# State-space angles made on POOL beside the feed-forward up stages and stored in DRAM; the direct products' table loads issued one piece ahead

## The reference

```python
# end of layer 0
x = x + squared_relu_mlp(rms_norm(x, norm_ffn[0]), ffn_up[0], ffn_down[0])   # 2048 -> 8192 -> 2048
# start of layer 1
u = rms_norm(x, norm_mix[1]) @ odd_w_in                 # 2048 x 2048
lam_bar = exp(lam * dt)                                 # one complex number per group and state
b_bar = ((lam_bar - 1) / lam)[..., None] * complex(b_re, b_im)
# states s[t] = lam_bar * s[t-1] + b_bar u[t];  y = Re(C s[t]) + d * u
z = gelu(y);  out = z * sigmoid(z @ w_glu + b_glu)
```

## Time and profile before

| | us |
|---|---|
| median of 3 runs | 4051.99 |
| lowest, highest | 4051.15, 4053.29 |
| the profiled execution's own time | 4037.2 |
| its span | 4035.9 |
| TensorE busy | 3800.0 (94%) |
| VectorE busy | 2590.0 (64%) |
| GpSimd busy | 1482.6 (37%) |
| ScalarE busy | 1790.8 (44%) |

### The profile page before, as it was taken

The page is one execution under the profiler, slowest core; times in us unless marked ns, Lnnn a source line. Parts: engine busy times, 40 slices in busy tenths (PEclk is TensorE's granted clock), DMA queues, the critical chain, the costliest instruction groups (busy, mean ns, idle before and its releaser), DMA issues.

```text
span 4035.9 us, 66394 instructions
## 1 busy us (share of the span) xinstructions
PE 3800.0 (94%) x28364; PEld 3232.6 (80%) x28364; DVE 2590.0 (64%) x3604; ACT 1790.8 (44%) x2785; POOL 1482.6 (37%) x710
## 2 busy tenths in 40 slices
PE   6898999998998999989999999999879989999998
PEld 3786888787877887888778888888768878888887
DVE  0435743785368897669879667885746876455457
ACT  1435443644355444445544444444435553333334
POOL 0332343233322441004344444444634434444443
PEclk8999999999999999999999999999899999999999
DMA  9653665355542442015356465657334435444543
GB/s 394 266 225 146 247 253 210 139 190 190 219 188 107 183 176 111 23 57 197 138 182 236 185 232 198 231 195 290 124 129 193 182 131 188 188 188 188 188 185 128
DMA packets 60663, 748.78 MB, mean 186 GB/s; under 512 B 6976, under 2 KB 9152, under 8 KB 16720
## 3 DMA queue, kind: packets, MB, share of 16 engines
q1 hardware_dynamic: 48960, 696.74, 45.2%
q0 software_dynamic: 9344, 45.69, 3.0%
q10 hardware_dynamic: 2064, 2.10, 0.1%
HBM read 727.65 MB, written 16.84 MB: 184 GB/s over the span
## 4 chain that ended last, share of the span: by engine, by line
PE 76%; DVE 13%; ACT 6%; DMA 3%; issue 2%; POOL 1%; SPq 0%; another core or an unknown queue 0%; DVEq 0%; ACTq 0%; POOLq 0%
PE ps L370 42%; PE ps L371 21%; DVE pieces L323 2%; DMA ring<-in_ada 2%; ACT pieces L307 2%; PE ps L2229 2%; PE ps L790 2%; DVE opa L571 1%; DVE r L1173 1%; PE ps L1899 1%; DMA s5u<-in_s5bt 1%; PE ps L3596 1%; DVE scr L592 1%; PE ps L3566 1%; PE ps L1044 1%
## 5 line engine op out<-in xcount | busy, mean ns | idle before, releaser
L370 PE MATMUL ps<-opa,pieces 128*128 128x512 f32 x6192 | 2250.1, 406 | 60.8 <-DVE pieces L323 36.5
L341 POOL TENSOR_TENSOR pieces<-ring,pieces 128x1024 fp32r<-128x1024 f32 x539 | 1345.1, 2496 | 2200.3 <-ACT pieces L307 2188.2
L371 PE MATMUL ps<-opa,pieces 128*128 128x256 f32 x6192 | 1740.1, 281 | 0.0
L307 ACT ACTIVATE pieces<-ring 128x1024 fp32r<-128x1024 f32 (+1 forms) x1110 | 1098.4, 1036 | 814.4 <-PE ps L371 813.9
L370 PEld LDWEIGHTS ps<-opa,pieces 128*128 128x128 f32 x6192 | 1171.3, 189 | 354.7 <-issue 40.6
L371 PEld LDWEIGHTS ps<-opa,pieces 128*128 128x128 f32 x6192 | 1177.6, 190 | 9.0 <-issue 5.3
L370 PE MATMUL ps<-opb,pieces 128*128 128x512 f32 x2560 | 907.9, 396 | 19.6 <-DVE pieces L323 13.8
L323 DVE TENSOR_TENSOR pieces<-ring,pieces 128x1024 fp32r<-128x1024 f32 (+1 forms) x571 | 724.5, 1269 | 272.0 <-ACT pieces L307 268.9
L371 PE MATMUL ps<-opb,pieces 128*128 128x256 f32 x2560 | 724.8, 283 | 0.0
L370 PEld LDWEIGHTS ps<-opb,pieces 128*128 128x128 f32 x2560 | 482.1, 188 | 141.4 <-issue 16.0
L371 PEld LDWEIGHTS ps<-opb,pieces 128*128 128x128 f32 x2560 | 482.6, 189 | 0.1
(11 more groups left out here) (425 smaller groups left out, 3345.2 us busy)
## 6 DMA issues: line engine op xcount, KB each, us to landing
ring<-in_up SPq DMA_DIRECT2D x64, 2048.0 KB, 7.7
ring<-in_down SPq DMA_DIRECT2D x64, 2048.0 KB, 7.7
ring<-in_win SPq DMA_DIRECT2D x56, 2048.0 KB, 7.7
ring<-in_ada SPq DMA_DIRECT2D x48, 2048.0 KB, 12.1
ring<-in_wout SPq DMA_DIRECT2D x24, 2048.0 KB, 7.7
ring<-in_evin SPq DMA_DIRECT2D x18, 2048.0 KB, 7.8
ring<-in_evout SPq DMA_DIRECT2D x8, 2048.0 KB, 8.0
ring<-in_xkv SPq DMA_DIRECT2D x8, 2048.0 KB, 7.6
```

Of the source, the lines that this page charges most:

```text
L307: a.do.activation(K.parts_of(p)[0][:, s, :], w[:, s, :], ACT.Copy).then_inc(*K.hi.up((p, h)))
L341: g.do.tensor_tensor(lo[:, s, :], w[:, s, :], hi[:, s, :].bitcast(F), ALU.subtract).then_inc(*K.lo2.up(p))
L370: pe.do.matmul(b[:, 0:512], hi[:, k, :], op[:, 512 * k:512 * k + 512], start=i == 0, stop=False)
L371: t = pe.do.matmul(b[:, 0:256], lo[:, k, :], half(op, 0, k), start=False, stop=i == kt - 1)
```

## The change

The angles are made earlier, and each is stored in DRAM. `pool_s5_angle` now makes one step's angles (256 elements) in two turns: a multiply and a two-operation rounding add (what ACT did before), then the subtraction of the large number, the difference, and a 128 KB store into a new DRAM tensor `s5_angles`. Its scratch is `cross5`, which DVE's table products use too. `pool_s5_beside` takes one turn after each `pool_feed` with t//16 equal to 2 or 4, the second and third up stages: 8 angles in each. A new angle waits until the store of the one before has landed. DVE's table products wait for angles 7 and 15 at two places, POOL for DVE's at two. ACT loads the angles back by pairs (`act_s5_angle`), and no longer makes `act_s5_whole`. POOL's queue in `pool_s5` holds only the products p.

Three smaller parts: the first direct product's tables are loaded at t = 112, the start of the last down stage's pieces, where they were loaded after the last one; the loads for the third and fourth direct product stand one piece earlier on POOL; and the first `pe_s5_in` comes after tile 12, the second waits for DVE's tile 13 only, with the PSUM banks handed out to fit.

```diff
+T_AFTER_ANGLES = {(2, 1, 0): 7, (4, 0, 1): 15}
+T_BEFORE_ANGLES = {0: (2, 0, 1), 8: (4, 0, 0)}
+def pool_s5_angle(K, n):
+    g = K.g
+    aq, at = K.cross5[:, 0:256], K.cross5[:, 256:512]
+    if n == 0:
+        g.wait_ge(*K.load["io5"].of("io5"))
+        g.wait_ge(*K.dve.of("ph"))
+    else:
+        g.wait_ge(*K.turned.of(("angle5", n - 1)))
+    if n in T_BEFORE_ANGLES:
+        g.wait_ge(*K.dve.of(("table", *T_BEFORE_ANGLES[n])))
...
+    g.do.tensor_tensor(r3(aq, 4), four, turn, ALU.mult).then_inc(*K.gps.up())
+    g.wait_ge(*K.gps.now())
+    g.do.tensor_scalar(at, aq, 1.0, MAG, ALU.mult, ALU.add).then_inc(*K.gps.up())
+    yield
+    g.wait_ge(*K.gps.now())
+    g.do.tensor_scalar(at, at, -MAG, None, ALU.add).then_inc(*K.gps.up())
+    g.wait_ge(*K.gps.now())
+    g.do.tensor_tensor(aq, aq, at, ALU.subtract).then_inc(*K.gps.up())
+    g.wait_ge(*K.gps.now())
+    g.do.dma_start(K.D["s5an"][n // 2][:, 256 * (n % 2):256 * (n % 2) + 256], aq).then_inc(*K.turned.up(("angle5", n), 16))
+    yield
+def act_s5_angle(K, m):
+    a = K.a
+    if m >= 2:
+        a.wait_ge(*K.act.of(("sin", 2 * m - 3)))
+    a.do.dma_start(K.an5[m % 2], K.D["s5an"][m]).then_inc(*K.load["an%d" % (m % 2)].up(("an", m), 16))
@@ def dve_s5_table(K, j):
+            if (j, c, h) in T_AFTER_ANGLES:
+                v.wait_ge(*K.turned.of(("angle5", T_AFTER_ANGLES[j, c, h])))
@@ def pool_s5_beside(K):
+    angles = chain.from_iterable(pool_s5_angle(K, n) for n in range(16))
     for t in range(2, 128):
...
+        if t == 112:
+            kept_all(K, g)
+            load_k(K, g, 2)
         pool_feed(K, p + t)
+        if t // 16 in (2, 4):
+            next(angles)
@@ def pool_odin(K):
-    kept_all(K, g)
-    load_k(K, g, 2)
...
     load_k(K, g, 3)
-    pool_feed(K, p + 5)
+    pool_feed(K, p + 4)
     g.wait_ge(*K.prod.of(("K", 3)))
     load_k(K, g, 1)
-    pool_feed(K, p + 8)
+    pool_feed(K, p + 7)
     g.wait_ge(*K.prod.of(("K", 1)))
     load_k(K, g, 0)
     pool_feed(K, p + 11)
-    pool_s5_angle(K, 0)
...
-    pool_s5_angle(K, 1)
@@ def pe_odin(K):
-        if n == 11:
+        if n == 12:
...
             pe_s5_in(K, 0)
@@ def act_odin(K):
-        if n in (12, 13):
-            act_s5_whole(K, n - 12)
+        if n == 10:
+            a.wait_ge(*K.prod.of(("K", 0)))
+            a.wait_ge(*K.turned.of(("angle5", 15)))
+            act_s5_angle(K, 0)
+            act_s5_angle(K, 1)
...
+        if n == 14:
+            act_s5_angle(K, 2)
@@ def pe_s5(K):
+    K.pe.wait_ge(*K.dve.of(("u", 13)))
+    pe_s5_in(K, 1)
     K.pe.wait_ge(*K.dve.of(("u", 15)))
-    pe_s5_in(K, 1)
@@ def act_s5(K):
-        if n % 2 == 0:
-            act_s5_whole(K, n // 2)
         act_s5_tables(K, n)
+        if n % 2 and n < 13:
+            act_s5_angle(K, n // 2 + 2)
@@ def pool_s5(K):
     for n in range(16):
-        if n % 2 and (n + 3) // 2 < 8:
-            pool_s5_angle(K, (n + 3) // 2)
```

More of the change, by code:

```diff
@@ L4 @@
 from contextlib import ExitStack
+from itertools import chain
 F = mybir.dt.float32
@@ L147, in begin @@
         for s in [self.tile, self.prod, self.hi, self.lo, self.lo2, self.act, self.dve, self.gps, self.stored,
-                  *self.landed, *self.kept, *self.load.values()]:
+                  *self.landed, *self.kept, self.turned, *self.load.values()]:
             s.n = 0
@@ L3204, in dve_s5_columns @@
     tt(fi, fi, ph2, ALU.mult, "fi")
+T_AFTER_ANGLES = {(2, 1, 0): 7, (4, 0, 1): 15}
[10 more added lines that the diff above has]
+        g.wait_ge(*K.dve.of(("table", *T_BEFORE_ANGLES[n])))
+    four = in_fours(K.io5)[:, :, 0][:, None, :].broadcast_to([P, 4, 64])
+    turn = of_step(K.ph5, n)[:, 0, :, None].broadcast_to([P, 4, 64])
+    g.do.tensor_tensor(r3(aq, 4), four, turn, ALU.mult).then_inc(*K.gps.up())
[14 more added lines that the diff above has]
+    a.do.dma_start(K.an5[m % 2], K.D["s5an"][m]).then_inc(*K.load["an%d" % (m % 2)].up(("an", m), 16))
 def dve_s5_table(K, j):
@@ L3225, in dve_s5_table @@
     if j:
-        v.wait_ge(*K.dve.of(("table", j - 1)))
+        v.wait_ge(*K.dve.of(("table", j - 1, 1, 1)))
     if j >= 2:
@@ L3236, in dve_s5_table @@
             v.wait_ge(*K.dve.now())
+            if (j, c, h) in T_AFTER_ANGLES:
+                v.wait_ge(*K.turned.of(("angle5", T_AFTER_ANGLES[j, c, h])))
             v.do.tensor_tensor(T, src[1 - c][:, s], b[:, s], ALU.mult).then_inc(*K.dve.up())
             v.wait_ge(*K.dve.now())
-            v.do.tensor_tensor(dst[c][:, s], dst[c][:, s], T, ALU.add if c else ALU.subtract).then_inc(*K.dve.up(("table", j)))
+            v.do.tensor_tensor(dst[c][:, s], dst[c][:, s], T, ALU.add if c else ALU.subtract).then_inc(*K.dve.up(("table", j, c, h)))
             yield
@@ L3246, in act_s5_pads @@
     which, k = TABLES[j]
-    a.wait_ge(*K.dve.of(("table", j)))
+    a.wait_ge(*K.dve.of(("table", j, 1, 1)))
     a.wait_ge(*K.dve.of("half5"))
@@ L3436, in pe_odin @@
             pe_s5_direct(K, ORDER_K[n])
-        if n == 11:
+        if n == 12:
+            at = K.ps.index(K.bank["tile", K.first["odin"] + 10])
+            K.z5b = Banks([K.ps[i] for i in (3, 4, 5, 6, 7, at)])
+            K.y5b = Banks([K.ps[i] for i in range(3) if i != at])
             K.pe.wait_ge(*K.act.of(("K", 0)))
@@ L3495, in of_step @@
     return a.rearrange("p (m q) -> p q m", q=4)[:, n % 4:n % 4 + d, n // 4 * 4:n // 4 * 4 + 4]
[L3498 to L3506, removed]
-    turn = of_step(K.ph5, 2 * m, 2)[:, :, :, None].broadcast_to([P, 2, 4, 64])
-    g.do.tensor_tensor(K.aq.rearrange("p (d m k) -> p d m k", d=2, m=4), four, turn, ALU.mult).then_inc(*K.gps.up(("turn5", m)))
-    g.wait_ge(*K.act.of(("whole5", m)))
-    g.do.tensor_scalar(K.at5, K.at5, -MAG, None, ALU.add).then_inc(*K.gps.up())
-    g.wait_ge(*K.gps.now())
-    if m >= 2:
-        g.wait_ge(*K.act.of(("tab", 2 * m - 3)))
-    g.do.tensor_tensor(K.an5[m % 2], K.aq, K.at5, ALU.subtract).then_inc(*K.gps.up(("angle5", m)))
-def act_s5_whole(K, m):
-    K.a.wait_ge(*K.gps.of(("turn5", m)))
-    K.a.do.activation(K.at5, K.aq, ACT.Copy, scale=1.0, bias=MAG).then_inc(*K.act.up(("whole5", m)))
 def act_s5_tables(K, n):
     a, an, sq, c, rt = K.a, K.an5[n // 2 % 2][:, 256 * (n % 2):256 * (n % 2) + 256], K.sq5[n % 2], K.cs5[n % 3], K.rt5[n % 3]
-    a.wait_ge(*K.gps.of(("angle5", n // 2)))
+    a.wait_ge(*K.load["an%d" % (n // 2 % 2)].of(("an", n // 2)))
     if n < 3:
@@ L3532, in act_s5_tables @@
     a.do.activation(c[:, 256:512], an, ACT.Sin, scale=-6.283185).then_inc(*K.act.up())
-    a.do.activation(sq, an, ACT.Sin, scale=3.1415925).then_inc(*K.act.up())
+    a.do.activation(sq, an, ACT.Sin, scale=3.1415925).then_inc(*K.act.up(("sin", n)))
     a.wait_ge(*K.act.now())
```

5 lines of the change are left out of this document (3 added, 2 removed).

## The result

| | before | changed |
|---|---|---|
| median of 20 runs, us | 4048.9 | 4058.8 |
| lowest, highest | 4036.99, 4054.46 | 4051.16, 4067.88 |
| the profiled execution, its span | 4037.2, 4035.9 | 4054.04, 4052.7 |

The ratio is 1.0023, with a 95% interval of 1.0016 to 1.0031: slower. The medians differ by 9.9 us; the interval means 6.5 to 12.6. The profiled execution of before lies 11.7 under its median and that of the changed kernel 4.8, so the two traces differ by more (16.8) than the kernels do. Most of the surplus of 6.9 will be found in one step of the output stage.

The account below looks back on a forecast made before the run. TensorE, 76% of the chain, was taken as the bound, so its waits count. Gains of 7.6 us against a loss of 11.6 gave +4.0: 4041 for the profiled execution, 4056 us as median, range 4045 to 4066.

Parts of the forecast that it names:

- The loads, 5.8: Direct products: earlier loads remove TensorE waits of 3.2 and 1.4 us and 1.2 of slow clock, a 5.8 us gain.
- The scan, 1.8: Output stage: with angle operations gone from between the products p, the first output step starts 1.8 us sooner.
- fourth rival: The scan's gain of 1.8 us goes only to another TensorE wait; within the range, no separate chance given.
- The clock in the second input step: Second input step, after the wait for its table: stays at half clock, 13.58 us where the first took 7.30.
- rival 2: Clock does not fall in the table wait, 2 us more gained; with early stores and no loss 4042, chance 0.08.
- Moving the input steps: First input step after tile 12, second after DVE's tile 13: costs nothing and changes nothing while the table lands last.
- The store's landing: Up stages: an angle store issued in mid-slab lands with the slab, 7.8 us after the split's end, or slightly later.
- The one-input operation: POOL's operation in the store's turn: hardly holds DVE up, unlike a two-input one, so it costs 0.
- The loss, 5.8 a stage: Second and third up stages: new angles waiting for stores lengthen POOL's loop, 11.6 us for two; bounds 0 to 19.
- slack of 1.4: Up stages: room in the POOL and DVE loop at the stage's start, 1.4 us, used up before anything is lost.
- Rival 3: POOL's loop costs more, from an excess of 1.6 us a pair: 16 us and more, 4060 to 4067, chance 0.23.
- The turn with a store costs 0: Up stages, odd tiles: one-input add, difference and store right after POOL's split cost 0.

Follow-up runs that it names:

- e2_loads: The kernel before with only the moved loads of the direct products, angles as before; 4042.1 us, ratio to before 0.9982.
- e11_loads: The same kernel as e2_loads, timed again in a later batch; 4042.4 us, ratio to before 0.9986.
- e3_late: The changed kernel with the direct products' loads back where they were before; 4061.7 us, ratio to before 1.0032.
- e9_turn_after: e1_swap with the new angle's multiply also waiting for DVE's square of the tile just ended; 4042.2 us, ratio to before 0.9984.
- e1_swap: The changed kernel with scratch halves swapped from angle to angle, the store's wait moved ahead of the odd tile's one-input operation; 4050.8 us, ratio to before 1.0007.
- e5_late_turn: e1_swap with the multiply waiting for DVE's square one tile too early, so it started as before; 4054.6 us, ratio to before 1.0010.
- e7_phase: The changed kernel with angle turns one tile later, stores issued in tiles without a slab's load; 4047.5 us, ratio to before 0.9996.
- e4_wait: The changed kernel without the multiply and first one-input operation of 14 angles, waits and stores kept; 4042.6 us, ratio to before 0.9987.
- e10_both: e7_phase with the multiply also waiting for DVE's square, no scratch swap; 4045.8 us, ratio to before 0.9992.

## Why the prediction was right, and where it was off

- **Direction: right; the size in part by luck.** 4056 was forecast and 4058.8 measured, but the forecast was +4.0 on a median of 4052.0, and the change was +9.9 on one of 4048.9. The kernel before came out 3.1 us lower than in its first three runs, and this hid half of what the sum missed. The loops that it named are the ones that the trace shows. (Its upper end of 4066 does not follow from a loss of 19 and a gain of 7.6, which give 4063; the time lies within either.)
- **The loads, 5.8: right**, 6.9 and 6.7 in e2_loads and e11_loads. In the traces the changed kernel comes to this stage 17.4 us late, reaches the first product 14.1 late (2781.78 against 2767.70), the third 11.1 late and the stage's last tile 10.0 late: 3.3 for the first wait, 3.0 for the slow clock and the second wait, 1.1 that I had not counted, of which e2_loads shows 0.6. The slabs that the loads passed lost nothing.
- **The scan, 1.8: right up to the first output step, and not shown beyond it.** Product to output is 19.4 to 21.4 us in the nine profiles with the angles elsewhere and 22.3 to 23.0 in the four without. But from the last tile of the input product to the next product's first tile it is 123.2 to 129.6 us in those nine and 121.5 to 128.3 in those four, with medians of 125.9 and 126.2. Nor do the medians of the times settle it. What is left for the scan when the loss and the loads' 6.8 (none in e3_late) are taken off is 2.9 us in e9_turn_after and 0 in e1_swap, and over all eight kernels with the angles elsewhere it runs from -2.5 (e5_late_turn) to 5.2 (e7_phase), with -0.6 for the changed kernel. The prediction's fourth rival, that this gain only goes to another wait, stays open.
- **The clock in the second input step: right.** It took 12.41 us and the granted clock was 0.52 from 2884 to 2894, the 1.2 GHz level; rival 2 did not come.
- **Moving the input steps: nothing, as said.** The second one now waits 2.76 us for DVE's scans (L3663) and not for its table; it starts 2.8 us after the last tile and started 2.4 after it before.
- **The store's landing: right in the middle, for the right reason.** 6.1 us, 8.2 after the split's end, beside the slab's 8.0. The Trainium skill's rule that an engine takes turns between its queues (DMA: Bandwidth & Descriptors, "Queues, rings and completion order") would have let it land early; 91 packets of the slab and none of the store's in 3.5 us do not agree, and only the last 38 of the slab's were mixed with them.
- **The one-input operation: right in size, and not for the reason given.** It cost DVE's two-input operation 0.08, the multiply 0.42. The prediction took the number of inputs to make the difference. By the rows of e1_swap it is the time that POOL's operation had left when the square began, 0.06 and 0.39. The Trainium skill's rule of the shared port pair (SBUF — State Buffer, "SBUF: two separate sides"), by which the one that starts first holds the pair for its whole instruction, agrees with both. The prediction let that rule cost 0.5 in each store's turn, 7 us in all; with the operation's 0.40 it would cost 0.06. Its own rows did not speak against the rule either: all eight of the L3510 took 1.49 us or more, so none shows what it takes alone. Twice 0.40 for its 512 elements would be an end at 2909.64, as the scans began; this is an estimate from L3227.
- **The loss, 5.8 a stage: mis-sized.** It was 8.0 with the down stage behind it (16.1 and 15.7 for two), and 7.8 and 6.6 in the up stages alone. The term that was too small is "the excess is 0.6 to 1.7 for each pair of tiles, 1.2 in the middle, in 6 pairs". The excess was 1.34 in most pairs (12.65 less 11.31; some took 12.4, one 13.0), and 7 angles of each stage wait, not 6: 9.4, and 8.0 when the slack of 1.4 is taken off. That is an upper value for the up stages; the next term was not in the sum at all. Rival 3 asked for an excess of 1.6, which did not come; its loss of 16 did, through the seventh pair and the down stages.
- **A term that was missing: the first tiles of the down stage.** There DVE's table operations ran beside POOL's splits, and TensorE waited for DVE's split. Timeline of POOL and DVE in the changed kernel, then TensorE's waits from 2306 to 2340 (before, 0.6 in one wait):

```profile
2318.20 2.45 POOL L342 TENSOR_TENSOR pieces<-ring,pieces 128x1024 fp32r<-128x1024 f32 x1 [0.36 <-ACT pieces L308]
2318.43 2.77 DVE L3280 TENSOR_TENSOR mix<-mix,scr 128x512 f32<-128x512 f32 x1
...
2323.76 2.92 DVE L3280 TENSOR_TENSOR mix<-mix,scr 128x512 f32<-128x512 f32 x1
```
```profile
PE ps L371 <- DVE pieces L324: 2.2, 2, 1.6
```

  L3280 took 2.8 and 2.9 us, and 0.69 in the same place of the kernel before. It costs 0.7 to 1.1 a stage and stays in the mildest variants: by TensorE's timeline the down stages take 1.1 us longer each in e4_wait and e9_turn_after, which is most of what these two lose. The wait for angle 7 was not it: the first table operation (L3278, 2315.50) followed DVE's split without a pause. Which of the two engines' operations starts first decides here, 0.23 us apart; that it comes out otherwise than before was seen and not changed by an experiment. The prediction gave "0, at worst 2 each" to this place for that wait.
- **"The turn with a store costs 0": right.** e4_wait keeps it, and two tiles take 11.45 for 11.38.
- **What the prediction did not see** is how the pair divides. It priced the multiply's hold on DVE at 0.4 a pair, less the whole slack, 0 to 3 for both stages. Without the wait it was 8.5. The slack of 1.4 is not free for the new work: the loop before already used it up at 0.07 a pair (11.38 for 11.31), and with 0.42 more and 0.08 for the store's turn the pair came to 11.87, 0.56 over TensorE's pace: 4.5 in eight pairs, and an up stage lost 3.6 (so the slack took 0.9, by difference), the down stage behind it 0.7.

So the loss came to 16 for the 11.6 forecast, and what the whole gained, by the medians, to 6 for 7.6: together +9.9 in place of +4.0. The lower median of the kernel before takes 3.1 of these 5.9 back, and 4056 is 2.8 too low.

## What to carry to other kernels

Where the loop of small operations between two engines is as long as the matmuls that it feeds, POOL's idle time is not room: price new work by the period of the loop, with each operation placed so that it isn't under way when the other engine's two-input operation starts, and take the period from two like instructions of POOL's, one round apart. A buffer that is stored and then written again wants one turn between, or its halves swapped; where a store must be waited for, issue it in the part of the rhythm in which no large transfer has just been issued. And move loads by themselves first: here they alone were the whole gain. Last, compare a change with a second profile of the kernel before: one step of this one took 7.9 us in one profile and 13.9 in the next.

## What the runs showed of the hardware

- A 128 KB store landed in 2.1 us with the queues empty and in 6.1 when issued 2.0 us after a 2 MB load; its packets did not move for the first 3.5 us.
- POOL standing still for 0.82 us ahead of a two-input operation made the pair of tiles 0.4 us shorter (11.45 for 11.87).
- A two-input operation of DVE's that takes 0.42 us alone took 0.84 when it began with about 0.39 us of an operation of POOL's still to run, and 0.50 with about 0.06.
- One program does its fourth input step in 7.9 us or in 13.9. Windows in the two profiles of before (length, busy of TensorE and its weight load, DVE, ACT, POOL, granted clock, DMA share, GB/s): the 2.4 GHz level in the first, the 1.2 GHz level in the second. What decides it was not found.

```profile
2931.00:2938.00 7.00, 6.95 (x243) 6.81 (x241) 0.55 (x2) 1.26 (x4) 2.76 (x2) 1.00 0.02 5
```
```profile
2934.00:2946.00 12.00, 12.00 (x232) 12.00 (x232) 0.14 (x1) 0.00 (x0) 2.75 (x2) 0.50 0.01 3
```

- A load ahead of a direct product, issued by POOL among slabs, landed after 11.5 us in the middle in the changed kernel; the chain of e10_both has one of 15.8, and TensorE waited. It was the second product, whose pair of loads the change leaves where it stood on POOL; of the thirteen profiles only this one shows that wait, and why the load took so long was not found.

```profile
2783.18 15.78 DMA s5u<-in_s5bt
```
